# Five more pairs of column chunks of the input projection from seven block products each

## The reference

```
h    = rmsnorm(x, norm1_w)                      # 288 x 1024
proj = h @ w_in                                 # 1024 x 6672
u_pool, u_qkv, b_raw, a_raw, z, gate_pool, gate_delta = split(proj)
q, k, v = split(silu(causal_conv(u_qkv)))       # 8 heads of 128
o    = gated_delta_chunked(l2norm(q), l2norm(k), v, g, beta, state)
o    = rmsnorm(o, o_norm_w) * silu(z)
merged = sigmoid(gate_pool) * (y_pool @ w_branch_pool) + sigmoid(gate_delta) * (o @ w_branch_delta)
x    = x + merged @ w_out
x    = x + hier_moe(rmsnorm(x, norm2_w), ...)   # 32 experts, 96 MB of weights
```

## Time and profile before

| what | value |
|---|---|
| median of 3 runs | 606.71 us (604.72 to 606.78) |
| profiled execution | 605.1 us, its span 603.4 us |
| PE busy | 546.1 us (91%) |
| DVE, ACT, POOL busy | 271.8, 147.0, 135.2 us |
| granted TensorE clock, mean | 0.972 of full speed |
| transferred | 158.59 MB, 263 GB/s over the span |

### The profile page before, as it was taken

The page is one execution under the profiler, slowest core; times in us unless marked ns, Lnnn a source line. Parts: engine busy times, 40 slices in busy tenths (PEclk is TensorE's granted clock), DMA queues, the critical chain, the costliest instruction groups (busy, mean ns, idle before and its releaser), DMA issues.

```text
span 603.4 us, 12000 instructions
## 1 busy us (share of the span) xinstructions
PE 546.1 (91%) x4820; PEld 407.7 (68%) x4820; DVE 271.8 (45%) x754; ACT 147.0 (24%) x389; POOL 135.2 (22%) x228
## 2 busy tenths in 40 slices
PE   8999999999999999988899999999596958699873
PEld 7899999777877755668789888756262626266431
DVE  4667667755343426145645344641404040405034
ACT  3367465237720001032100123101000101000112
POOL 5777774121200540006204422200000000000000
PEclk9999999999999999999999999999889888989997
DMA  9755444839933274442387863999999999999992
GB/s 234 238 159 150 153 141 141 281 120 328 296 102 118 64 244 130 150 144 66 104 261 304 351 253 128 378 422 421 410 420 420 420 420 421 420 419 421 419 361 79
DMA packets 82582, 158.59 MB, mean 263 GB/s; under 512 B 11245, under 2 KB 65274, under 8 KB 70849
## 3 DMA queue, kind: packets, MB, share of 16 engines
q1 hardware_dynamic: 79724, 154.22, 69.8%
q10 hardware_dynamic: 2805, 3.62, 2.0%
HBM read 150.05 MB, written 7.96 MB: 262 GB/s over the span
## 4 chain that ended last, share of the span: by engine, by line
PE 70%; DMA 21%; SPq 3%; DVE 3%; issue 1%; ACT 0%; POOL 0%; DVEq 0%; POOLq 0%
PE ps L1358 21%; DMA arena<-in_w_up_dram 19%; PE ps L1367 13%; PE ps L2011 7%; PE ps L1879 5%; PE ps L1828 3%; PE ps L1311 3%; PE ps L1781 3%; SPq L654 2%; DMA arena<-in_w_down_dram 2%; SPq L581 1%; PE ps L1821 1%; PE ps L1564 1%; PE ps L1528 1%; PE ps L2086 1%
## 5 line engine op out<-in xcount | busy, mean ns | idle before, releaser
L1358 PE MATMUL ps<-arena 128*128 128x288 f32 x480 | 130.1, 416 | 0.7 <-DVE arena L2202 0.7
L1358 PEld LDWEIGHTS ps<-arena 128*128 128x128 f32 x480 | 87.1, 190 | 26.5 <-issue 3.1
L2011 PE MATMUL ps<-arena 128*32 128x256 f32 x1024 | 65.3, 414 | 31.2 <-DMA arena<-in_w_up_dram 29.8
L1367 PE MATMUL ps<-arena 128*128 128x144 f32 x616 | 78.3, 287 | 0.0
L1367 PEld LDWEIGHTS ps<-arena 128*128 128x128 f32 x616 | 76.3, 190 | 2.4 <-issue 1.9
L2011 PEld LDWEIGHTS ps<-arena 128*32 128x32 f32 x1024 | 38.2, 119 | 56.8 <-issue 42.1
L2227 DVE SCALAR_TENSOR_TENSOR ps<-arena,ps 128x312 f32<-128x312 f32 x72 | 39.1, 545 | 2.4 <-ACT ps L1019 0.9
L2023 PE MATMUL ps<-arena 128*128 128x128 f32 x336 | 38.7, 275 | 0.0
L2023 PEld LDWEIGHTS ps<-arena 128*128 128x128 f32 x336 | 38.1, 192 | 0.4 <-DVE arena L2896 0.4
L2086 PE MATMUL ps<-arena 128*128 128x512 f32 x64 | 31.2, 618 | 1.9 <-ACT arena L1256 1.0
L2917 DVE TENSOR_TENSOR arena<-arena,ps 128x256 f32<-128x256 f32 x8 | 3.4, 422 | 65.0 <-issue 36.8
(11 more groups left out here) (410 smaller groups left out, 749.3 us busy)
## 6 DMA issues: line engine op xcount, KB each, us to landing
arena<-in_w_up_dram SPq DMA_DIRECT2D x32, 1024.0 KB, 17.5
arena<-in_w_gate_dram SPq DMA_DIRECT2D x28, 1024.0 KB, 19.0
arena<-in_w_down_dram SPq DMA_DIRECT2D x28, 1024.0 KB, 19.0
arena<-in_w_in_dram SPq DMA_DIRECT2D x26, 1024.0 KB, 6.7
out_dram<-arena SPq DMA_DIRECT2D x9, 512.0 KB, 7.1
arena<-in_w_branch_delta_dram SPq DMA_DIRECT2D x4, 1024.0 KB, 6.1
arena<-in_w_out_dram SPq DMA_DIRECT2D x4, 1024.0 KB, 5.4
arena<-in_w_gate_dram SPq DMA_DIRECT2D x8, 512.0 KB, 9.6
```

What stands on the lines that cost most here:

```text
L1358: last = mm(ps[n % 2][:, 0:T], w[:, k, P * (n % 2):P * (n % 2) + P], hT[:, k, :], start=(k == 0), stop=(k == KD - 1))
L1367: last = mm(to[:, 0:HT], left[:, k, :], right[:, k, :], start=(first and k == 0), stop=(k == HK - 1), skip_group_check=True)
L2011: last = mm(to[CAP * e:CAP * e + CAP, 0:FE], xgT[u][:, k, CAP * e:CAP * e + CAP], w[e][:, k, :], start=(k == 0), stop=(k == KD - 1))
```

## The change

Items 15 to 19 (z chunks 2 to 7, gates 0 to 3) become fast pairs. Their results are added in place, in the rows of `zT` and `gT` where they end, and ACT takes the curve there, the half-chunks from PSUM and from SBUF. The products of one head stand inside each pair, those of the next behind it; `sample_tiles` and `state_products` move with them, and `sample_tiles(7)` and `(8)` come one chunk later, behind chunks 40 and 41. Slots 4 and 5 hold sums until item 23, so items 12 to 23 use four slots; SP's other work moves two items earlier in its list, so that it stands between loads of the same place in the ring's time. POOL gets five groups of weight sums at written places in its list. Dt and egq get a second buffer. DVE's `prep` is cut into three parts. New on PE: the wait for `wp_ev` (the pool branch's rows, from ACT) ahead of all five pairs, which was inside `prep` of head 0. The diff, without the lines that only rename FAST:

```diff
-FAST = range(1, NQKV // 2)
+QKV_FAST = range(1, NQKV // 2)
+Z_FAST = range(15, 20)
+FAST = [*QKV_FAST, *Z_FAST]
...
-SLOT_OF = [i % 4 if i < NQKV // 2 else i % RA for i in range(A_ITEMS)]
+SLOT_OF = [i % 4 if i < 24 else i % RA for i in range(A_ITEMS)]
...
-CONV_AT = NQKV // 2 + RA
-ROWS_AT = NQKV // 2 + RA
-DIAG_AT = (N_GATE + 2) // 2 + RA - 1
+CONV_AT = NQKV // 2 + 4
+ROWS_AT = NQKV // 2 + 4
+DIAG_AT = (N_GATE + 2) // 2 + 3
...
+Dts, egqs = (Dt, wk.take(TP)), (egq, wk.take(P))
...
-    free[n] = (free[n - 1] if n else 0) + (1 if n // 2 in FAST else 2 if n < N_POOL else 3 if n < N_Z else 1)
+    free[n] = (free[n - 1] if n else 0) + ((3 if n % 2 else 1) if n // 2 in Z_FAST else 1 if n // 2 in FAST else 2 if n < N_POOL else 3 if n < N_Z else 1)
...
+def pair_rows(i):
+    n = 2 * i
+    if n < N_GATE:
+        return zT[:, n - N_Z, :], zT[:, n - N_Z + 1, :]
+    return gT[:, n - N_GATE, :], gT[:, n - N_GATE + 1, :]
...
-        if i == RA + 15:
+        if i == 19:
             sp.wait_ge(S["memsets"], 1)
             sp.dma_start(x_image, X[:, 0:2 * H * TILE]).then_inc(S["diag"], 16)
...
-    sum_weights(FAST[0])
...
+    sum_weights(15)
...
     row_masks()
     nc.gpsimd.memset(XT, 0.0).then_inc(S["memsets"], 1)
+    sum_weights(16)
     pool.wait_ge(S["diag"], 16)
     own_columns(0)
+    sum_weights(17)
+    sum_weights(18)
     pool.wait_ge(S["sd_pe"], 1)
     own_columns(1)
+    sum_weights(19)
     pool.wait_ge(S["sd_pe"], 2)
     nc.gpsimd.memset(X[:, 2 * H * TILE:6 * H * TILE], 0.0).then_inc(S["memsets"], 1)
...
-        nc.scalar.activation(egq, aqT[:, 2 * h + 1, :], ACT.Exp).then_inc(S["expd"], 1)
+        nc.scalar.activation(egqs[h % 2], aqT[:, 2 * h + 1, :], ACT.Exp).then_inc(S["expd"], 1)
...
-            v = Dt[:, P * c:P * c + P]
+            v = Dts[h % 2][:, P * c:P * c + P]
...
-    for h in range(H):
-        rows_exp(h)
-        if h == 1:
+    def first_of_pair(i):
+        d0, d1 = pair_rows(i)
+        act.wait_ge(S["proj"], product(i, P1))
+        nc.scalar.activation(d0[:, HT:T], ps[0][:, 0:HT], ACT.Copy).then_inc(S["proj_free"], 1)
+    def curve(to, src, i):
+        if 2 * i < N_GATE:
+            nc.scalar.activation(to, src, ACT.Silu).then_inc(S["proj_free"], 1)
+        else:
+            nc.scalar.activation(to, src, ACT.Tanh, scale=0.5).then_inc(S["proj_free"], 1)
+    def pair_curves(i):
+        d0, d1 = pair_rows(i)
+        act.wait_ge(S["proj"], product(i, P2))
+        curve(d0[:, 0:HT], ps[0][:, 0:HT], i)
+        act.wait_ge(S["sums"], added(i, SUM5))
+        curve(d0[:, HT:T], d0[:, HT:T], i)
+        act.wait_ge(S["sums"], added(i, SUM6))
+        curve(d1, d1, i)
+    for i in Z_FAST:
+        h = 2 * (i - Z_FAST[0])
+        if h < H:
+            rows_exp(h)
+        first_of_pair(i)
+        if h < H:
+            rows_exp(h + 1)
+        if h == 2:
             act.wait_ge(S["decdve"], 1)
             nc.scalar.activation(Dq, Dq, ACT.Exp).then_inc(S["dec_act"], 1)
-        evac(N_Z + Z_AHEAD + h)
-    evac(N_Z + Z_AHEAD + H)
-    for n in range(N_GATE + 3, N_GATE + LEAD_GATES):
+        pair_curves(i)
+    for n in range(2 * Z_FAST[-1] + 2, N_GATE + LEAD_GATES):
         evac(n)
...
-            pe.wait_ge(S["proj_free"], free[n - 2 if item - 1 not in FAST else 2 * item - 1])
+            pe.wait_ge(S["proj_free"], free[n - 2] if item - 1 not in FAST else free[2 * item - 2] + 1)
...
-    def fast_pair(i, between):
+    def fast_pair(i, between, banks=(ps[0], ps[1], ps[4], ps[5])):
...
-        pe.wait_ge(S["proj_free"], free[2 * i - 1])
-        block_product(ps[0], a11, b11)
+        a, b_, c, d = banks
+        pe.wait_ge(S["proj_free"], free[2 * i - 2] + 1 if i - 1 in FAST else free[2 * i - 1])
+        block_product(a, a11, b11)
         if i == FAST[0]:
             pe.wait_ge(S["ht_done"], KD + 4)
         pe.wait_ge(S["pads"], weights_summed(i, 2))
-        block_product(ps[1], s2, t2_)
-        if i != FAST[0]:
+        block_product(b_, s2, t2_)
+        if i - 1 in FAST:
             pe.wait_ge(S["sums"], added(i - 1, SUM5))
-        else:
+        elif i == FAST[0]:
             pe.wait_ge(S["small_ev"], 4)
-        block_product(ps[4], s1, t1_)
+        block_product(c, s1, t1_)
         between()
         pe.wait_ge(S["pads"], weights_summed(i, 3))
-        if i != FAST[0]:
+        if i - 1 in FAST:
             pe.wait_ge(S["sums"], added(i - 1, SUM6))
-        block_product(ps[5], s3, t3_)
+        block_product(d, s3, t3_)
         pe.wait_ge(S["proj_free"], free[2 * i])
-        block_product(ps[0], a12, b21, first=False)
+        block_product(a, a12, b21, first=False)
         pe.wait_ge(S["pads"], weights_summed(i, 4))
         pe.wait_ge(S["sums"], added(i, SUM4))
-        block_product(ps[4], s4, b22, first=False)
+        block_product(c, s4, b22, first=False)
         pe.wait_ge(S["sums"], added(i, SUM7))
-        block_product(ps[5], a22, t4_, first=False)
+        block_product(d, a22, t4_, first=False)
...
-    for h in range(H):
-        proj(N_Z + Z_AHEAD + h)
-        prep(h)
+    pe.wait_ge(S["wp_ev"], NG)
+    def between_pairs(i):
+        h = 2 * (i - Z_FAST[0])
+        if h < H:
+            prep(h)
+        if h == 4:
+            sample_tiles(2, 0, TS, Nq, lambda own, j: ident[own, own])
+        if h == 6:
+            sample_tiles(4, 0, TS, IAq, lambda own, j: N2q[own, j, :])
+        if h == H:
+            state_products(1)
+    for i in Z_FAST:
+        h = 2 * (i - Z_FAST[0])
+        fast_pair(i, lambda: between_pairs(i), (ps[0], ps[1], ps[3], ps[4]))
+        if h < H:
+            prep(h + 1)
         if h == 0:
             sample_rows()
-        if h == 2:
-            sample_tiles(2, 0, TS, Nq, lambda own, j: ident[own, own])
-        if h == 3:
+        if h == 4:
+            state_products(0)
             sample_tiles(3, 2 * TS, TS, tq, lambda own, j: Nq[own, j, :])
-        if h == 4:
-            sample_tiles(4, 0, TS, IAq, lambda own, j: N2q[own, j, :])
-            state_products(0)
-        if h == 5:
+        if h == 6:
             sample_flips()
-    proj(N_Z + Z_AHEAD + H)
-    state_products(1)
-    for n in range(N_GATE + 3, N_GATE + LEAD_GATES):
+    for n in range(2 * Z_FAST[-1] + 2, N_GATE + LEAD_GATES):
         proj(n)
-        if n == N_GATE + 3:
+        if n == N_GATE + 4:
             sample_tiles(7, 0, P, TTq, lambda own, j: Rq[own, j, :])
-        if n == N_GATE + 4:
+        if n == N_GATE + 5:
             sample_tiles(8, 2 * P, P, aqq, lambda own, j: vnq[own, j, :])
...
-    def prep(h):
-        products = ps[5 + h % 2]
+    def decays_of(h):
         if h == 0:
             dve.wait_ge(S["row_dma"], 16 * 3)
-        V.tensor_tensor(Dt.rearrange("p (c t) -> p c t", c=2), aqT[:, 2 * h:2 * h + 2, :],
+        if h >= 2:
+            dve.wait_ge(S["prep_done"], h - 1)
+        V.tensor_tensor(Dts[h % 2].rearrange("p (c t) -> p c t", c=2), aqT[:, 2 * h:2 * h + 2, :],
                         above.unsqueeze(1).to_broadcast([P, 2, P]), ALU.add).then_inc(S["dt"], 1)
+    def betas_of(h):
         dve.wait_ge(S["expd"], 3 * h + 3)
         v = AT[:, 2 * h:2 * h + 2, :]
-        link(V.tensor_tensor(v, v, Dt.rearrange("p (c t) -> p c t", c=2), ALU.mult))
+        link(V.tensor_tensor(v, v, Dts[h % 2].rearrange("p (c t) -> p c t", c=2), ALU.mult))
+    def prep(h):
+        products, dt = ps[5 + h % 2], Dts[h % 2]
         dve.wait_ge(S["qk_pe"], h + 1)
         for c in range(2):
-            for j, (to, by) in enumerate(((aqT, Dt[:, P * c:P * c + P]), (AT, AT[:, 2 * h + c, :]))):
+            for j, (to, by) in enumerate(((aqT, dt[:, P * c:P * c + P]), (AT, AT[:, 2 * h + c, :]))):
                 ins = V.scalar_tensor_tensor(to[:, 2 * h + c, :], products[:, TP * c + P * j:TP * c + P * j + P],
                                              rqk[:, c, H + h:H + h + 1], by, ALU.mult, ALU.mult)
         link(ins)
-        V.tensor_tensor(qkvT[:, h, P:TP], qkvT[:, h, P:TP], egq, ALU.mult).then_inc(S["prep_done"], 1)
+        V.tensor_tensor(qkvT[:, h, P:TP], qkvT[:, h, P:TP], egqs[h % 2], ALU.mult).then_inc(S["prep_done"], 1)
+    def pair_u2(i):
+        d0, d1 = pair_rows(i)
+        dve.wait_ge(S["proj_free"], free[2 * i])
+        dve.wait_ge(S["proj"], product(i, P6))
+        V.tensor_tensor(d1[:, 0:HT], d0[:, HT:T], ps[1][:, 0:HT], ALU.add).then_inc(S["sums"], 1)
+    def pair_u4(i):
+        d0, d1 = pair_rows(i)
+        dve.wait_ge(S["proj"], product(i, P5))
+        dve.wait_ge(S["sums"], added(i, SUM2))
+        V.tensor_tensor(d1[:, HT:T], d1[:, 0:HT], ps[3][:, 0:HT], ALU.add).then_inc(S["sums"], 1)
+    def pair_u7(i):
+        d0, d1 = pair_rows(i)
+        dve.wait_ge(S["proj"], product(i, P7))
+        dve.wait_ge(S["sums"], added(i, SUM4))
+        V.tensor_tensor(d1[:, HT:T], d1[:, HT:T], ps[4][:, 0:HT], ALU.add).then_inc(S["sums"], 1)
+    def pair_u5(i):
+        d0, d1 = pair_rows(i)
+        dve.wait_ge(S["proj"], product(i, P3))
```

(56 more changed lines are left out.)

## The result

The changed kernel took 615.8 us in the median of 4 runs (614.14 to 618.56), the kernel before 606.4 us on the same chip: a ratio of 1.0161 [1.014, 1.0183], 9.4 us slower. The forecast was 613.0, and the range to 615.5 missed it by 0.3.

The account below looks back on a forecast made before the run. PE was taken to bound the stage. Losses 0.7 + 1.7 + 5.5 + 1.5 + 0.3 + 1.2, less 4.5 won, rounding 0.1, made it 6.3 us later: median 606.71 becomes 613.0, with an 8-in-10 range of 605.2 to 615.5.

Parts of the forecast that it names:

- the clock: Behind PE's wait in pair 17: the granted clock falls to half, costing 1.5 us, ends 0 and 2.8.
- The second sum of item 17: POOL's list: queued behind the wait for late zeros, it ends at 160.8, while PE wants it at 155.3.
- anchored, whatever happened before: PE from 160.8 on: times follow from that release; sample_tiles(7) can start at 197.65, 7.2 us later than before.
- The hole: PE ahead of P6 of pair 17: stands still 5.5 us for POOL's second sum, with nothing to cover it.
- The wait for SUM7: Pair 15: SUM7 comes from DVE at about 142.9, PE wants P4 at 141.1; cost about 1.7 us, between 0 and 2.5.
- the wait for ACT's copy: Pair 15: the first additions need this copy, which stands behind head 0's exponentials; no separate PE cost was given.
- The 0.7 for the pool rows: PE ahead of the pairs: waits for ACT's last pool branch rows, done at 134.2; cost 0.7 us.
- the 0.3 for SUM7 in pair 18: DVE operations slowed beside POOL's sums for item 19 make PE wait; cost 0.3 us, ends 0 and 1.7.
- The round trip: Diagonal blocks: later sample tiles delay the fetch to 219.1, while PE comes at 217.9 and waits 1.2 us.
- POOL in time: Rival: PE never waits for POOL's sums, 1.0 us gained, 605.7 us; chance 0.13.
- The whole saving: Rival: also nothing waits in pair 15 or for ACT, 3.5 us gained, 603.2 us; chance 0.04.
- Item 23: Rival: this first load behind the diagonal blocks comes late, PE waits 5.4 us more, 618.4 us; chance 0.07.

Follow-up runs that it names:

- e1: Changed kernel with POOL's weight sums for item 17 moved ahead of its wait for the zeros; 610.3 us, ratio 1.0065.
- e8: Changed kernel with only a new order of ACT, DVE and PE work in pair 15, item 17's sums left in place; 616.9 us, ratio 1.0167.
- e6: e1 plus another order in pair 15 and no PE wait for the pool rows ahead of the pairs; 606.9 us, ratio 1.0023.
- e5: e1 plus sample_tiles(7) directly behind the last pair, (8) behind chunk 40, and DVE's part ahead of them inside that pair; 607.39 us, ratio 1.0029.
- e7: Changed kernel with the edits of e1, e5 and e6 joined; 605.65 us, ratio 0.9986.
- e9: e7 with DVE's pair sums, for which PE waits, ahead of the head's scaling; 604.17 us, ratio 0.9974.
- e2: Changed kernel with 14 idle products of constants on PE ahead of its wait for POOL in pair 17; 613.86 us, ratio 1.0127.
- e3: Kernel before with only sample_tiles(7) and (8) one chunk later in PE's list; 608.87 us, ratio 1.0055.
- e10: The same kernel as e7 once more, on another chip; 604.89 us, ratio 0.9983.

## Why the prediction was right, and where it was wrong

The mechanism came out as forecast; two terms of the sum were too small, the clock and a wait that stood at nothing, and the time fell out of the range by them.

**The direction, the mechanism and its place** were right. The second sum of item 17 was forecast for 160.8, and it ended at 161.94 less 1.12 = 160.8. To hit it so well is in part luck, since the zeros' landing scatters by 1.4 us over the traces. That they land late because they stand behind the state loads was not tested; no run moved them. POOL is the releaser. e1 shows that this queue order costs 5.5 us with the clock it takes, e8 that it is an anchor, as "anchored, whatever happened before" said.

**The hole** was put at 5.5 us and is 3.8. The error is in pair 15, and cancels: PE came 1.8 us later than the 155.3 of the text (162.00 - 3.82 - 1.12 = 157.1). The wait for SUM7 was sized 1.7 and is 2.19, and the wait for ACT's copy, put at nothing, is 0.55; the rest is spread. The 0.7 for the pool rows is 0.64, and the 0.3 for SUM7 in pair 18, with POOL beside DVE, is 0.17 (184.63).

**The clock** is the first failed term: 1.5 us taken, from the row behind 5.71 us of waiting, and 2.9 measured, just past the upper end of 2.8. The failed step is the choice of the row by the length of the pause. What PE loses is half of the time that it then works at half clock, and that time doesn't follow the pause's length. Two windows of the experts' stage, in the trace of before, show when the clock came back behind the two pauses of the earlier trace rows (columns as above):

```profile
443.00:444.00 1.00, 1.00 (x20) 0.46 (x12) 0.00 (x0) 0.00 (x0) 0.00 (x0) 0.78 1.02 426
...
470.00:471.00 1.00, 1.00 (x20) 0.52 (x16) 0.00 (x0) 0.00 (x0) 0.00 (x0) 0.62 1.02 426
```

From the restart of PE to there (estimates from the windows' clocks) it is 3.0 us behind the pause of 5.71, where 1.5 were lost, and 5.6 behind that of 7.69, where 2.8 were. In the changed kernel it is 5.9 us behind a pause of 3.82, for the 2.9; in e8 5.0 behind 7.76; and in e1 3.4 us at half clock follow a pause of 2.47. So the row that the text kept for its upper end was the closer one, though its pause was the longer. From the anchor to tiles 7 the text has 197.65 + 1.8 - 160.8 = 38.65 us; the trace has 202.50 - 161.94 = 40.56, 1.9 more, of which the clock is 1.4.

**The round trip** was right in kind and size: PE waits 0.94 at L1683 for the 1.2 forecast, and the fetch lands at 222.0 - 1.1 = 220.9, later than 219.1 by 1.8, which are those 1.9 but for rounding.

**The wait before L1672** is the second failed term. It stood in no step: 1.17 us between the last interleaved product and the first state unit, with no releaser in the trace; the kernel before has none there. It appears only with a late fetch (also 0.64 in e1, 1.18 in e6, 1.48 in e8) and is away when the tiles are early (e5, e7, e9). But e2 and e3 have the late fetch without it. The DMA views give a lead: in each of the four traces with this wait one packet of the instruction queue (q8, 0.02 MB) stands some 2.4 to 2.7 us before the first product of L1672, however long the wait; in the other eight none stands within the 3.8 us before it. That fits PE waiting for its own instructions, but no run tests it, and the cause stays open.

Together 1.9 + 1.2 = 3.1 us too little, against 615.8 - 613.0 = 2.8.

**The rivals.** POOL in time was priced at 605.7, and e1, which makes just that true, took 610.3. Its price left out 2.5 + 0.4 us of pair 15's waits against the 1.7 taken, the half clock behind them (the head's products 1.91 us there too), and 1.5 us of the fetch and L1672: 1.2 + 1.6 + 1.5 = 4.3 of the 4.6 us between the two. The whole saving, 603.2, was reached to within 1 us only by e9. Item 23 was not late: PE has no wait for a load there. The error in width follows from the same omission: the upper end added 1.3 for the clock and nearly 1.4 for POOL beside DVE, but nothing for a wait not yet seen.

## What to carry to other kernels

When an edit adds work to an engine that was idle, read that engine's list in order, and find the wait that stands ahead of the new work: a one-line move of the sums ahead of an unrelated wait gave back 5.5 of 9.4 us. Where such a queue holds another engine, price everything from the moment it releases it: savings before that moment are worth nothing (e8), while one behind it shows in the time (e2). A faster product on PE pays only as far as the engines that add its pieces keep up, so put the sums that PE waits for ahead of work that it doesn't wait for yet.

## What the runs showed of the hardware

A pause of PE of nearly the same length cost the clock in one run and not in another. In the changed kernel's trace PE waits 2.19 us before 145.49, and the head's products behind it take 1.03 us, at full clock. In e1 it waits 2.47 us at the same place, and they take 1.91:

```profile
143.97 1.46 PE L1409 MATMUL ps<-arena 128*128 128x144 f32 x8 [2.47 <-DVE arena L2526]
145.22 1.91 PE L1571 MATMUL ps<-arena 128*128 128x256 f32 x4
```

e2 (2.20 us, full clock) and e5 (2.46 us, half) repeat the two cases, so the 0.3 us of length can be the reason as well as the moment at which the pause fell. One kernel can differ with itself, too: e7 and e10 are the same program, and the first projection starts at 13.04 partly at half clock in one (8.58 us) and at 12.49 at full clock in the other (8.00 us).

The Trainium skill, "TensorE: Matmul & The Clock Gate", Part 1, says that the hardware judges PE's activity in windows that run on by themselves and don't begin with the kernel, so that the moment at which the clock changes varies from run to run. The first projection of e7 and e10 agrees with that; the two pauses don't decide it.

The longer pause of e8, 7.76 us, lost no more behind it than that of 3.82: the 16 products that follow take 4.21 us in both, and the head's products 1.52 and 1.91. It is the work behind a pause that pays, until the clock is back, and filling the pause with idle products (e2) took the price away.

With a weight sum of POOL beside it, a DVE operation with both inputs in SBUF takes 1.31 to 1.37 us instead of 0.29 to 0.42, and POOL's sum 1.45 instead of 1.26 (1.34 and 1.45 at 141.09 and 142.40 in the changed kernel). Both take longer there, DVE far more.
